# Differential attention and retention gate: Silu replaced by Tanh and a VectorE product, single score banks for short units

## The reference

```
proj = rms_norm(x) @ w_in             # 2560 columns: q, k, v of 4 heads; q, k, v, gate of the retention; pool
s = q_m k_m^T / 8  (two maps m per head), causal;  p_m = softmax(s)
a = p_1 - lambda * p_2;  o_da = rms_norm(a @ v)
ret = (o - mean) * rsqrt(var + eps) * ret_g
o_ret = silu(g) * ret                 # the gate
mix = concat(o_da, o_ret, o_pool) @ w_out
```

## Time and profile before

| | us |
|---|---|
| median of 3 runs | 3939.26 (3938.01 to 3941.7) |
| the profiled execution | 3940.71 |
| its span | 3938.9 |
| PE busy | 3742.0 (95%) |
| DVE busy | 2230.0 (57%) |
| POOL busy | 1918.0 (49%) |
| ACT busy | 1452.8 (37%) |

### The profile page before, as it was taken

The page is one execution under the profiler, slowest core; times in us unless marked ns, Lnnn a source line. Parts: engine busy times, 40 slices in busy tenths (PEclk is TensorE's granted clock), DMA queues, the critical chain, the costliest instruction groups (busy, mean ns, idle before and its releaser), DMA issues.

```text
span 3938.9 us, 49604 instructions
## 1 busy us (share of the span) xinstructions
PE 3742.0 (95%) x19015; PEld 3092.7 (79%) x19015; DVE 2230.0 (57%) x3538; ACT 1452.8 (37%) x2930; POOL 1918.0 (49%) x1675
## 2 busy tenths in 40 slices
PE   5899999999999999999898999999999898999998
PEld 4788888787888877787676888888877676888887
DVE  5333334645777766534638777534544638777533
ACT  1123232225666652225534333212225534333211
POOL 1414132742333326321526778986321526788975
PEclk8999999999999999999999999999999899999999
DMA  5322222221000003200132222544110132222543
GB/s 179 112 72 87 63 64 88 95 80 35 8 9 9 6 33 104 63 26 11 32 124 72 83 88 81 190 145 144 50 37 14 32 124 68 83 83 83 184 160 124
DMA packets 245062, 309.84 MB, mean 79 GB/s; under 512 B 38533, under 2 KB 156693, under 8 KB 244826
## 3 DMA queue, kind: packets, MB, share of 16 engines
q1 hardware_dynamic: 212152, 231.87, 19.0%
q10 hardware_dynamic: 32674, 74.80, 5.5%
HBM read 252.96 MB, written 51.53 MB: 77 GB/s over the span
## 4 chain that ended last, share of the span: by engine, by line
PE 75%; DVE 15%; ACT 4%; issue 3%; POOL 2%; DMA 1%; ACTq 0%; DVEq 0%; SPq 0%; POOLq 0%
PE ps L130 71%; PE ps L133 4%; DVE ml_p L142 3%; DVE cst_sm L153 3%; ACT thi L136 2%; DVE tlo L142 1%; DVE f_ta L150 1%; ACT ml_o L136 1%; DVE f_tb L150 1%; POOL mix_z L142 1%; ACT tfi L136 0%; POOL wlo L142 0%; POOL mlo_z L142 0%; DVE da_am L150 0%; DVE cst_sm L150 0%
## 5 line engine op out<-in xcount | busy, mean ns | idle before, releaser
L139 POOL CAST whi<-wst 128x512 fp32r<-128x512 f32 (+2 forms) x508 | 417.5, 822 | 1258.2 <-DMA wst<-in_a_w_in 384.3
L142 POOL TENSOR_TENSOR wlo<-wst,whi 128x512 fp32r<-128x512 f32 (+2 forms) x634 | 938.2, 1487 | 40.8
L130 PE MATMUL ps<-whi,thi 128*128 128x512 f32 (+3 forms) x1816 | 710.0, 391 | 17.8 <-POOL wlo L142 5.4
L130 PE MATMUL ps<-whi,tlo 128*128 128x512 f32 (+3 forms) x1816 | 686.0, 378 | 0.0
L130 PE MATMUL ps<-wlo,thi 128*128 128x512 f32 (+3 forms) x1816 | 684.6, 377 | 0.0
L130 PEld LDWEIGHTS ps<-whi,thi 128*128 128x128 f32 x1816 | 345.1, 190 | 80.7 <-POOL wlo L142 7.3
L130 PEld LDWEIGHTS ps<-wlo,thi 128*128 128x128 f32 x1816 | 345.1, 190 | 57.7 <-issue 4.1
L130 PEld LDWEIGHTS ps<-whi,tlo 128*128 128x128 f32 x1816 | 343.8, 189 | 58.1
L130 PE MATMUL ps<-thi,whi 128*128 128x512 f32 x856 | 342.0, 400 | 38.1 <-POOL wlo L142 28.4
L130 PE MATMUL ps<-tlo,whi 128*128 128x512 f32 x856 | 338.6, 396 | 0.0
L130 PE MATMUL ps<-thi,wlo 128*128 128x512 f32 x856 | 338.1, 395 | 0.0
(11 more groups left out here) (391 smaller groups left out, 8111.9 us busy)
## 6 DMA issues: line engine op xcount, KB each, us to landing
wst<-in_w_down SPq DMA_DIRECT2D x140, 256.0 KB, 3.3
wst<-in_w_up SPq DMA_DIRECT2D x126, 256.0 KB, 2.9
scr_h<-f_tb SPq DMA_DIRECT2D x44, 512.0 KB, 4.0
wst<-in_w_in SPq DMA_DIRECT2D x80, 256.0 KB, 2.7
wst<-in_a_w_in SPq DMA_DIRECT2D x72, 192.0 KB, 2.5
wst<-in_ada_w SPq DMA_DIRECT2D x48, 256.0 KB, 4.8
da_am<-in_ada_w SPq DMA_DIRECT2D x48, 256.0 KB, 2.6
f_T2lw<-scr_h SPq DMA_DIRECT2D x48, 256.0 KB, 3.8
```

The source lines that it names most:

```text
L130: return self.none if self.e is None else self.e.matmul(*a, **k)
L139: return self.none if self.e is None else self.e.tensor_copy(*a)
L142: return self.none if self.e is None else self.e.tensor_tensor(*a)
```

## The change

1. `act_fill` for n < 4 computes tanh(g/2) with scale 0.5 into `gr`, and no longer frees the bank. A new function `dve_fill` on VectorE computes (gr + 1) * g, with g still read from the PSUM bank, and frees the bank. It stands in step i after the two maxima of unit i, for the tile that was finished in step i-1: in steps 5, 7, 9 and 11.
2. In `dve_mix` the reciprocal deviations `vs` (128x32) of the retention are multiplied by 0.5, which supplies the missing half.
3. Units with j <= 3 (at most 512 keys) take their two banks from a new ring `s1` of the four single banks 0 to 3, so that a unit's two maps take banks 0 and 1, or 2 and 3. The maxima and exponentials read one bank instead of a slice of two. The data that they read is the same in size.

```diff
+    "s1": [(0,), (1,), (2,), (3,)]
...
         if n < 4:
-            ins = q.activation(self.gr[:, 2 * n:2 * n + 2, :], src.rearrange("p (a b) -> p a b", a=2), ACT.Silu)
+            q.activation(self.gr[:, 2 * n:2 * n + 2, :], src.rearrange("p (a b) -> p a b", a=2), ACT.Tanh, scale=0.5).then_inc(
+                *S.up("gexp", ("ret", l, n)))
+            return
...
+    def dve_fill(self, q, l, n):
+
+        key, g = ("fill", l, n), self.gr[:, 2 * n:2 * n + 2, :]
+        q.wait_ge(*self.S.at("gexp", ("ret", l, n)))
+        q.stt(g, g, 1.0, self.ps[:, self.B.of(key), :].rearrange("p (a b) -> p a b", a=2), ALU.add, ALU.mult).then_inc(
+            *self.B.free(key, "evac_v"))
...
+        q.tensor_scalar(self.vs, self.vs, 0.5, None, ALU.mult).then_inc(*S.up("v_seq"))
+        q.wait_ge(*S.last("v_seq"))
...
-        bs = [B.take(("cs", l, i, mp), "s2") for mp in range(2)]
+        bs = [B.take(("cs", l, i, mp), "s2" if j > 3 else "s1") for mp in range(2)]
...
-            q.activation(dst[:, 0:w, :], ps[:, b:b + 2, :].rearrange("p a (c e) -> p (a c) e", e=128)[:, 0:w, :], ACT.Exp,
+            q.activation(dst[:, 0:w, :], ps[:, b:b + -(-w // 4), :].rearrange("p a (c e) -> p (a c) e", e=128)[:, 0:w, :], ACT.Exp,
...
-                    q.tensor_reduce(self.cstat(i, 2 + mp), ps[:, b:b + 2, :].rearrange("p a b -> p (a b)")[:, 0:w], AXX,
+                    q.tensor_reduce(self.cstat(i, 2 + mp), ps[:, b:b + -(-w // 512), :].rearrange("p a b -> p (a b)")[:, 0:w], AXX,
                                     ALU.max, negate=True).then_inc(*S.up("c_max", (l, i, mp)))
+            if i and self.fill_at(i - 1) and self.fill_at(i - 1)[1] and self.fill_at(i - 1)[0] < 4:
+                self.dve_fill(q, l, self.fill_at(i - 1)[0])
```

More of the change, by code:

```diff
@@ L174 @@
 class Banks:
-    RINGS = {"proj": [(0,), (1,), (2,), (3,)], "tr4": [(4,), (5,), (6,), (7,)], "s2": [(0, 1), (2, 3)],
+    RINGS = {"proj": [(0,), (1,), (2,), (3,)], "tr4": [(4,), (5,), (6,), (7,)], "s2": [(0, 1), (2, 3)], "s1": [(0,), (1,), (2,), (3,)],
              "s3": [(0,), (1,)], "t3": [(2,), (3,)], "d3": [(4,), (5,)], "o3": [(6,)], "a3": [(7,)], "t2": [(4,), (5,)], "o2": [(6,), (7,)],
```

## The result

| | before | changed |
|---|---|---|
| median of 7 runs, us | 3941.70 (3938.01 to 3945.70) | 3949.75 (3947.57 to 3953.09) |
| ratio, with its 95% interval | | 1.0022 (1.0012 to 1.0031) |
| profiled execution, us | 3940.71 | 3951.12 |

The change makes the kernel 8.05 us slower by the medians, +0.2%. The forecast was +6.9 us, 3946.2 from the first median of 3939.26; on the median of all seven runs of before it would be 3948.6. The time lies in the range of 3940 to 3950.5. Whether the change is over or under 0.2% can't be told: the interval of the ratio is 4.7 to 12.2 us.

What follows compares the result with a forecast made beforehand. PE, busy 95% of the span, was taken as the bound. Its new waits, 2.1 + 1.35 + 2.10 + 1.36 = +6.9 us, with all other terms 0, put the median of 3939.26 at 3946.2 us, range 3940 to 3950.5.

Steps and rivals of the forecast that it cites:

- PE waits for the bank in steps 9 and 11, not in 5 and 7: Fill steps: VectorE's later readout makes PE wait 2.1 and 1.35 us in layer 0, 2.10 and 1.36 in layer 1.
- Table loads worth at most 0.25 us in all: ScalarE beside PE's full stretch: dropping 20.5 us of loads gains 0, at most the 0.25 us that PE idles there.
- Halving: 0: One 128x32 VectorE operation per layer, taken as 0.3 us, hidden by 2.09 us of idle before the first unit's maxima.
- The meeting with GpSimd's products: 0: Fill steps: gate products beside VectorE's 128x1 product and mix cause PE no wait: 0, at most 0.5 us a layer.
- The clock holds: Fill steps: PE, full on both sides of the new waits, keeps full clock; the forecast's own case, chance 0.50.
- one of the signs that I had named for being wrong: Wrong if PE's new waits are below 1 us, the clock there is under 1.00, or the tail moves over 2 us.
- Rival 1: New waits pull PE's clock down, 1.7 us a fall; 3947.9 with one, 3949.6 with one in each layer; chance 0.27.
- Single banks: 0: Score banks: nothing waits for the earlier scores in the tail, so 0; bounds -2.7 to +0.5 us a layer.
- Rival 3: The tail gets shorter by the single banks, 2.7 us a layer, giving 3940.8 us; chance 0.16.
- rival 2: ScalarE was the hidden bound in the fill stretches; 20.5 us of table loads come back, giving 3925.7 us; chance 0.04.
- rival 4: Fill bank isn't waited for as forecast, because VectorE's order leaves the product early enough: 3939.5 us; chance 0.03.
- The bound in the tail: Tail: VectorE and ScalarE answer each other; PE's scores are ready before VectorE comes to them.

## Why the prediction was right or wrong

- **PE waits for the bank in steps 9 and 11, not in 5 and 7**: right. Step 9 starts the fill 2.06 us later and step 11 1.32, where I had 2.1 and 1.35; steps 5 and 7 are unchanged to 0.01 us. The idle times in the trace, 1.82 and 1.08, are 0.25 shorter; the ends of matmuls are modelled, and I take it that they reach beyond the point at which the next could start. Moving the product and nothing else moves these waits as the rows say: none ahead of the maxima, fills 1.1 and 0.6 us later between them, and 3.7 and 3.3 behind the mix.
- **The product's duration**: 0.70 taken, 0.68 measured.
- **Table loads worth at most 0.25 us in all**: wrong, and the bound more than the value. They were worth 0.28 us a layer, 0.6 in all. I took PE's idle time as the upper end of the gain, but the wait of unit 10's second map lies inside a row of matmuls that counts as busy.
- **Halving: 0**: right. The operation takes 0.18 us, puts what follows it 0.21 us later (0.3 taken), and VectorE's idle time before the first maxima goes from 2.09 to 1.88.
- **The meeting with GpSimd's products: 0**: right. The 128x1 product grew to 0.78 or 0.79 us in each of the four steps of layer 0 and the mix from 1.28 to 1.74 in step 9 and from 1.02 to 1.46 in step 11. No step got longer by it.
- **The clock holds** in the likeliest case: this is the step that failed, and one of the signs that I had named for being wrong, a clock row under 1.00, came up (0.54). Rival 1 held in the profiled execution, with one fall in each layer as it had for 3949.6, and none behind the shorter waits of step 11. Its price of 1.7 us for a fall came out at 1.4 to 1.5. Its chance of 0.27 looks too low: three of four executions had a fall there, five of eight stretches. With no fall the change costs 2 * 3.14 = 6.3 us in these steps; five eighths of two falls at 1.5 add 1.9, which makes 8.2 against the 8.05 measured. That they agree so closely is luck: the interval of 4.7 to 12.2 would have taken the 6.3 alone as well, and the falls are shown by the traces, not by the medians. The waits themselves were forecast well: steps 9 and 11 are 3.42 us longer in a layer without a fall, 6.8 in all for the 6.9 of the sum. The table loads, which the sum had at 0, take 0.6 off again. I had argued that PE, full on both sides of the wait, would keep its clock. That doesn't decide it: the same 1.82 us wait was followed by a fall in some stretches and by none in others. What decides between them stays open; these stretches have the same work and differ in when they come in the execution.
- **Single banks: 0**: right. The steps and the tails show it, alone and left out; the medians only bound it to about 4 us. Rival 3 falls with that, rival 2 with the 0.6 us of the table loads, and rival 4 with the two waits a layer.
- **The bound in the tail** was named rightly (VectorE and ScalarE answering each other), but I did not ask what stood behind the waiting instruction on VectorE. There lay 15 us by the traces and 20 by the medians, about twice what the change cost.

## What to carry to other kernels

When a readout is moved from one engine to another, place it by when its buffer is wanted, not by where it fits: the same 0.68 us product cost nothing ahead of two reductions and 8 us behind them, because those first wait for the very engine that needs the buffer next. On an engine that works in order, look at what stands behind an instruction that waits. If it is ready and the waiting one isn't, exchange them: that gave 15 to 20 us here, while 20.5 us of table loads taken from ScalarE gave 0.6. A wait put into a stretch in which TensorE is full can cost more than its length: here the clock fell behind five of the eight waits of 1.8 us. And when two traces differ by 1.4 to 1.6 us in a stretch with the same text, look at the granted clock before looking for a cause in the edit.

## What the runs showed of the hardware

The granted clock fell for 3.4 us behind a wait of 1.8 us in five of eight stretches, and began to be low 0.9 to 1.6 us after TensorE had started again. It fell behind a wait of 1.58 us for `wlo` in one trace, behind none of the 1.4 us waits at that place in others, behind none of the eight waits of 1.1 us in step 11, and behind the waits of 0.8 us between the maxima in neither layer. Behind waits of up to 3.5 us, with the product last, it fell in both layers, for 3.4 us and once more for 6.8; the longer fall began 0.8 to 1.2 us before TensorE started again. A fall of 3.4 us in a full stretch cost 1.4 to 1.6 us, a little under half of it.

Much of the spread between runs of one kernel goes with this clock. Of the 31 runs of the kernel before in the first group, the five with a mean granted clock of 0.981 took 3936.0 us on average and the five with 0.977 took 3944.6.

A VectorE 128x1 product took 0.22 us alone and 0.78 to 0.79 us in each of layer 0's four steps in which GpSimd's two gate products of 128x256 started beside it, and a mix of 128x1024 took 1.74 instead of 1.28. The new product, with one operand in SBUF and one in PSUM, took 0.68 to 0.69 us at every place.
